# The modulation blocks at the head of a decoder layer loaded as two 1 MB transfers in a ring, in place of four of 512 KB

## The reference

```python
mod = jnp.dot(jax.nn.silu(c), w_ada[l]) + b_ada[l]        # c: 9 rows of 2048, w_ada: 2048 x 12288
sh1, sc1, g1, sh2, sc2, g2 = jnp.split(mod[:, None, :], N_MOD, axis=-1)
h = rmsnorm(x, g_mix[l]) * (1 + sc1) + sh1
z = jnp.dot(h, w_in[l])                                    # then attention, pooling and gated linear attention
x = x + g1 * jnp.dot(mix, w_out[l])
h2 = rmsnorm(x, g_ffn[l]) * (1 + sc2) + sh2
gate, up = jnp.split(jnp.dot(h2, w_gu[l]), 2, axis=-1)
x = x + g2 * jnp.dot(jax.nn.silu(gate) * up, w_down[l])
```

## Time and profile before

| | |
|---|---|
| median of 3 runs | 2471.78 us (2469.92 to 2472.15) |
| the profiled execution, its own time | 2467.32 us |
| its span, first to last instruction | 2465.5 us |
| PE / DVE / ACT / POOL busy | 95% / 63% / 37% / 10% of the span |
| DMA, mean over the span | 171 GB/s |
| bytes in the 64 whole rows | 33.6 MB |
| mean granted TensorE clock | 0.983 |

### The profile page before, as it was taken

How to read it: one execution, slowest core, us unless ns; L and a number is a source line. 1 busy time by engine, 2 the same in 40 slices (tenths; PEclk the granted TensorE clock), 3 DMA queues, 4 the chain that set the end, 5 groups by cost and what they waited for, 6 DMA issues and landing times.

```text
span 2465.5 us, 44142 instructions
## 1 busy us (share of the span) xinstructions
PE 2346.9 (95%) x18537; PEld 2182.4 (89%) x18537; DVE 1553.5 (63%) x2236; ACT 921.7 (37%) x1324; POOL 238.7 (10%) x285
## 2 busy tenths in 40 slices
PE   5689999999999899899999999999999989999996
PEld 1179888788787799899999999999999989999996
DVE  0342552323232422588888888888888788888898
ACT  2122442323232322544444444444444433333343
POOL 3150140000000111200000000000000211011131
PEclk9989999999999999999999999999999999999998
DMA  9955465555553434214434433443344586365562
GB/s 339 342 184 175 154 157 190 188 181 188 171 192 121 160 110 127 103 69 167 150 123 162 163 118 126 164 166 135 135 167 166 207 301 212 132 228 203 172 212 95
DMA packets 190949, 422.41 MB, mean 171 GB/s; under 512 B 14564, under 2 KB 116756, under 8 KB 188704
## 3 DMA queue, kind: packets, MB, share of 16 engines
q1 hardware_dynamic: 171072, 341.35, 40.4%
q0 software_dynamic: 17088, 73.78, 8.6%
q10 hardware_dynamic: 2592, 4.46, 0.5%
HBM read 365.45 MB, written 54.08 MB: 170 GB/s over the span
## 4 chain that ended last, share of the span: by engine, by line
PE 91%; DMA 3%; DVE 2%; issue 2%; ACT 1%; SPq 0%; POOL 0%; DVEq 0%; POOLq 0%; ACTq 0%
PE PJ L2290 27%; PE PS L2290 27%; PE PJ L1924 25%; DMA AR<-in_weights 3%; PE PJ L1877 2%; PE PJ L1867 1%; PE PJ L2255 1%; PE PS L2150 1%; PE PS L2181 1%; PE PS L2255 1%; PE PS L2174 1%; PE PJ L1889 1%; PE PJ L2232 1%; DVE X L1844 0%; PE PS L2153 0%
## 5 line engine op out<-in xcount | busy, mean ns | idle before, releaser
L2290 PE MATMUL PS<-HS,WO 128*128 128x272 f32 x5376 | 684.2, 289 | 10.3 <-issue 9.5
L2290 PEld LDWEIGHTS PS<-HS,WO 128*128 128x128 f32 x5376 | 679.4, 188 | 11.9 <-issue 11.9
L2290 PE MATMUL PJ<-HS,WO 128*128 128x272 f32 x5376 | 680.6, 288 | 0.0
L2290 PEld LDWEIGHTS PJ<-HS,WO 128*128 128x128 f32 x5376 | 677.3, 188 | 0.0
L1100 ACT ACTIVATE WO<-GR 128x1024 fp32r<-128x1024 f32 (+1 forms) x462 | 477.0, 1033 | 508.5 <-PE PS L2290 243.6
L1619 DVE TENSOR_TENSOR WO<-GR,WO 128x1024 fp32r<-128x1024 f32 (+1 forms) x462 | 556.2, 1204 | 117.6 <-ACT WO L1100 117.5
L1924 PE MATMUL PJ<-HH,WH 128*128 128x272 f32 x1568 | 348.1, 304 | 20.7 <-issue 7.9
L1924 PE MATMUL PJ<-HL,WH 128*128 128x272 f32 x1568 | 327.7, 291 | 0.0
L1924 PE MATMUL PJ<-HH,WL 128*128 128x272 f32 x1568 | 327.5, 291 | 0.0
L1259 DVE TENSOR_TENSOR WL<-RW,WH 128x1024 fp32r<-128x1024 f32 x102 | 129.4, 1273 | 285.5 <-ACT WH L839 285.2
L1924 PEld LDWEIGHTS PJ<-HH,WH 128*128 128x128 f32 x1568 | 248.7, 191 | 55.2 <-issue 43.3
(11 more groups left out here) (308 smaller groups left out, 1846.3 us busy)
## 6 DMA issues: line engine op xcount, KB each, us to landing
GR<-in_weights SPq DMA_DIRECT2D x264, 512.0 KB, 6.7
AR<-in_weights SPq DMA_DIRECT2D x256, 256.0 KB, 4.5
RW<-in_weights SPq DMA_DIRECT2D x102, 512.0 KB, 4.4
HS<-act_parts POOLq DMA_DIRECT2D x91, 544.0 KB, 5.9
act_parts<-SQ SPq DMA_DIRECT2D x40, 952.0 KB, 7.0
AR<-in_weights SPq DMA_DIRECT2D x64, 512.0 KB, 5.3
MIX<-in_xT SPq DMA_DIRECT2D x1, 4352.0 KB, 16.7
X<-in_xT POOLq DMA_DIRECT2D x4, 1088.0 KB, 10.1
```

What stands on the lines that cost most here:

```text
L2290: mm = e.matmul(out, w[part], HS[:, HS_AT[QUARTER[i]], y, (2 * first + k) % (KT // 2), :], start=OPENS[i] and k == 0 and x == 0, stop=k == ...
```

## The change

The ring memory stays where it is. It is seen as two buffers of two rows (`AR2[i]`, 128 x 2 x 1024), and a transfer fills one of them with rows n and n + 1 of a whole block: 1 MB, 32 transfers in place of 64. The transfer for rows n and n + 1 waits until both rows of its buffer have been used (`ada_used` >= n - 2). On TensorE both rows of a pair wait for the same semaphore. The half blocks go to the same addresses by the same transfers as before, and their waits count as before.

```diff
-    AR = [sb(f"AR{i}", [P, HU]) for i in range(AS)]
+    spot[0] += 4 * HU * AS
+    AR2 = [sb(f"AR2{i}", [P, 2, HU], at=ar_at + 8 * HU * i) for i in range(AS // 2)]
...
+        def load_ada_pair(n):
+
+            if n >= AS:
+                sp.wait_ge(S["ada_used"], n - AS + 2)
+            sp.dma_start(AR2[n % AS // 2][:, :, :], ins["weights"][n:n + 2].rearrange("r p n -> p r n"))\
+                .then_inc(ada_in[n % AS], 16)
+
         def load_ada(n):
             if n >= AS:
                 sp.wait_ge(S["ada_used"], n - AS + 1)
             at = ada_in[n % AS]
-            if n < ADA_V * A_FIRST:
-                sp.dma_start(AR[n % AS][:, :], ins["weights"][n]).then_inc(at, 16)
-                return
             x, s = divmod(n - ADA_V * A_FIRST, AS)
...
-        for n in range(ADA_V * A_FIRST):
+        for n in range(0, ADA_V * A_FIRST, 2):
             if n == AS:
                 sp.dma_start(MIX[:, :, :], ins["xT"]).then_inc(S["x_in"], 16)
             if n == ADA_V * (A_FIRST - 1):
                 for t in range(RAW):
                     load(At(t))
-            load_ada(n)
+            load_ada_pair(n)
...
         def ada_slot(n):
 
             whole = min(n // AS + 1, ADA_V * A_FIRST // AS)
-            e.wait_ge(ada_in[n % AS], 16 * whole + 32 * (n // AS + 1 - whole))
+            if n < ADA_V * A_FIRST:
+                e.wait_ge(ada_in[n % AS // 2 * 2], 16 * whole)
+            else:
+                e.wait_ge(ada_in[n % AS], (0 if n % 2 else 16 * whole) + 32 * (n // AS + 1 - whole))
...
-                    mm = e.matmul(PJ[j:j + CP, 2 * pair, :], CS[:, k, :], AR[n % AS][:, 512 * c:512 * c + 512],
+                    mm = e.matmul(PJ[j:j + CP, 2 * pair, :], CS[:, k, :], AR2[n % AS // 2][:, n % 2, 512 * c:512 * c + 512],
                                   start=(k < 4), stop=(k >= KT - 4))
```

More of the change, by code:

```diff
@@ L582, in load_ada @@
             for w in range(2):
-                sp.dma_start(AR[n % AS][:, 2 * HB * w:2 * HB * w + 2 * HB].rearrange("p (k n) -> p k n", k=2),
+                sp.dma_start(AR2[n % AS // 2][:, n % 2, 2 * HB * w:2 * HB * w + 2 * HB].rearrange("p (k n) -> p k n", k=2),
                              ins["weights"][r + w].rearrange("p (k n) -> p k n", k=2)[:, :, c:c + HB]).then_inc(at, 16)
@@ L1877, in ada_half @@
                     mm = e.matmul(PJ[CP * x:CP * x + CP, 2 * pair, 0:HB], CS[:, 4 * s + x, :],
-                                  AR[n % AS][:, HB * x:HB * x + HB], start=(s == 0), stop=(s == AS - 1))
+                                  AR2[n % AS // 2][:, n % 2, HB * x:HB * x + HB], start=(s == 0), stop=(s == AS - 1))
                 mm.then_inc(S["ada_used"], 1)
```

## The result

| | before | after |
|---|---|---|
| median of 8 runs | 2469.87 us (2464.72 to 2472.15) | 2480.02 us (2477.55 to 2483.32) |
| the profiled execution, its own time | 2467.32 us | 2479.6 us |
| its span | 2465.5 us | 2477.8 us |
| mean granted TensorE clock | 0.983 | 0.963 |

The ratio is 1.0044, with a 95% interval from 1.0035 to 1.0053: slower by 0.44%, 10.2 us.

The account below looks back on a forecast made before the run. It took the ring and TensorE, each waiting for the other, to bound the stage. Its terms 6.8 + 0.4 + 2.5 + 1.7 made +11.4 us, so 2483.2 us for the median, with a range of 2468 to 2490 us.

Parts of the forecast that it names:

- What bounds it: Ring and TensorE wait for each other, as in a ring too short for its cycle; ring transfers some 79 us of the chain.
- The clock: TensorE's granted clock while the ring is used in pairs: 1.2 GHz throughout, so a pair takes 1.95 us, not 1.08.
- the middle: Stretch from pair (8, 9) to pair (54, 55): 23 steps of 3.50 us against 3.203, +6.8 us.
- The cycle: One buffer's round: 4.9 us issue to landing, 1.95 use, 0.15 hand-overs, 7.0 us for two pairs.
- The two-row issue: SP's issue of one 1 MB transfer: 0.55 to 0.61 us against 0.33, the 0.22 us more counted in the landing.
- TensorE's other work: Turns at six block ends and `sum_x` get in the pairs' way: 4.5 us in all, somewhat over half counted, +2.5.
- Start: Beginning of the middle: pair (8, 9) lands at 31.6 against 31.21, +0.4 us.
- End: Rows behind the `RW` transfers: row 63 starts no later, but its use and turn last longer at 1.2 GHz, +1.7 us.
- The sum: All terms together: 6.8 + 0.4 + 2.5 + 1.7 = +11.4 us, 2478.7 for the profiled execution, 2483.2 for the median.
- Rival B: The clock stays or comes back: 3.07 us a pair, about 2470 us, no difference; chance 0.27, shared with rival D, unchanged pieces.
- Rival C: Larger transfers stream better: at 2.8 us a pair 9.3 us less, 2462.5 us; chance 0.11.

Follow-up runs that it names:

- the fourth experiment: The changed kernel with both rows of a pair in the same two column groups, one after the other; 2485.56 us, 1.0056 to the kernel before.
- the first experiment: The changed kernel plus one idle float32 matmul, whose result nothing reads, after each pair of rows; 2471.14 us, 1.0001 to the kernel before.
- e8: The changed kernel with four 1 MB buffers for all 64 rows and the six `RW` transfers behind row 63; 2446.47 us, 0.9897 to the kernel before.
- e9: e8 with the idle matmul added behind each pair; 2447.66 us, 0.9904 to the kernel before.

## Why the prediction was right

It worked out 2483.2 us for the median, slower the likeliest outcome, and it was 2480.02. Step by step:

- **What bounds it.** Right. The ring and TensorE wait for each other: holding a buffer longer (pairs at the low clock, the fourth experiment) made the stage longer, two more buffers of the same kind shortened it by 23 x (3.584 - 2.606) = 22.5 us.
- **The clock ("this term decides").** Right. It was 0.52 in the middle, pairs took 1.93 us (1.95 predicted), and one idle product a pair removed the loss. That pairs reopen the gap of each cycle is shown by the paired waits alone, at unchanged transfers. Whether rows side by side count as more work stays open, as it did in the prediction: the same eight instructions in 1.91 us one after the other kept the clock at 1.00 for 24 us, but not steadily before.
- **The cycle.** 4.9 + 1.95 + 0.15 = 7.0 predicted, 6.98 measured: 4.92 to landing, 2.00 from the pair's start to its release, 0.06 of hand-overs. The two-row issue was mis-sized: 0.37 us against 0.33, not 0.55 to 0.61. The strided half block was the wrong row to take it from. The premise that a transfer mostly starts when its forerunner has ended was wrong too: the other one is still under way at each issue (36.61, with the other landing before 38.97). That the landing was 4.9 us all the same is partly luck: of the 0.22 us that the issue was to add to 4.7, it added 0.04, and where the rest comes from is not shown.
- **TensorE's other work, +2.5.** The undisturbed step of 3.49 gives 23 x 0.29 = 6.6 of the middle's 8.8 us; 2.2 are left for turns and `sum_x`.
- **Start, +0.4.** It was +0.84, the term that was furthest off for its size. Pair (8, 9) started at 32.05, not 31.6; of these 0.45 us, 0.3 come from rows 4 and 5, whose use started at 25.04 and not at 24.75.
- **End, +1.7.** +1.63.
- **The sum.** 11.4 predicted to the first projection, 11.24 measured. That it fits so closely is luck in part: the middle was put 0.5 us too high (6.8 + 2.5, measured 8.8) and the start 0.4 too low. For the profiled execution 2478.7 was predicted and 2479.6 came; of the 3 us too many in the median, 1.9 lie in the starting value (2471.78 from three runs, 2469.87 from all eight) and 1.2 in the difference (11.4, measured 10.2).
- **Rival B** is the first experiment: the clock kept, no difference (2471.14). It named the right condition and nearly the right step. **Rival C** failed on its own condition: it wanted a landing under 4.4 us at full clock. With the clock kept, in the first experiment, the landing was 5.0 us in the median, the pairs 3.18 us apart, and 1 MB transfers gave 333 GB/s.

## What to carry to other kernels

When a ring is bound by its cycle, count the transfers in flight before making them larger: in fixed memory, larger ones halve that count and hold each buffer longer, while more memory (here borrowed from a buffer that is idle in that stage) brought the stream to the engines' rate. Grouping the waits of a matmul loop lengthens its gaps, so compare the granted clock and the durations of single instructions on both sides. Then look at what is queued ahead of the last transfers that the critical path needs.

## What the runs showed that was not expected

- A low clock costs nothing where the transfers bind (e8 and e9: 0.76 and 1.00, 2446.47 and 2447.66 us), and all of the loss where buffer and use form one cycle.
- 512 KB and 1 MB transfers move the same GB/s in a full queue (401 and 406), and, with 4 MB of buffers to fill in both, take nearly as long from issue to landing (7.9 and 8.3 us in the median).
- In the profile the clock of a stretch before the first clock record reads 1.00 even where MATMULs take 1061 ns (the run with paired waits).
- Three buffers of 1 MB, 1.5 times the memory, were not enough for the engines' rate, at a clock of 0.58: 2.954 us a pair, where four gave 2.606. Why is open.
